# The attention bias kept with reversed rows, and the mLSTM gates computed feature-major

## The reference

```python
yc, yl = even_mixer(hc @ ev_w_in, hl @ ev_w_in, na_rpb, ml_conv_w, ...)
# split of the 3088 columns: NA q, k, v | mLSTM x, v, o | i gates (8) | f gates (8)
# latent attention, per grid row of 64 tokens (4 rows):
s_loc = q . k_window + rpb[head, row offset, column offset]   # window of 16 columns
s_ctx = q . k_context
p = softmax([s_loc, s_ctx]);  out = p_loc . v_window + p_ctx . v_context
# mLSTM, per head (4) and direction (2):
i_pre = zi + i_bias;  log_f = log_sigmoid(zf + f_bias)
```

## Time and profile before

| | |
|---|---|
| median of three runs | 2040.75 us |
| the profiled execution's own time | 2040.45 us |
| its span in the profile | 2038.7 us |
| mean granted clock of TensorE | 0.974 of full speed |
| busy: PE, VectorE, ScalarE, GpSimd | 96%, 62%, 32%, 14% |

### The profile page before, as it was taken

One profiled execution on the slowest core, in us unless ns is written; L12 is line 12 of the kernel. 1 busy time (PEld: TensorE's weight loads), 2 busy tenths in 40 slices (PEclk: granted clock), 3 DMA queues, 4 the chain that ended last, 5 costly groups with the idle time before them and its releaser, 6 DMA issues.

```text
span 2038.7 us, 24301 instructions
## 1 busy us (share of the span) xinstructions
PE 1950.0 (96%) x9246; PEld 1535.7 (75%) x9246; DVE 1267.0 (62%) x2231; ACT 645.4 (32%) x1093; POOL 290.4 (14%) x318
## 2 busy tenths in 40 slices
PE   6999999999999989899999999999999899989997
PEld 6888878885554454688887888888778867779997
DVE  7677776753872663677678447774677535465454
ACT  2322242323342431422224233222432332324452
POOL 0000001240000002500000122000034535130003
PEclk9999999998997999899999999999999999989999
DMA  8354536313350001245544223553234555214442
GB/s 359 123 203 169 206 139 167 128 54 124 135 217 0 1 0 42 104 170 204 203 165 167 96 114 140 207 206 123 103 115 174 208 193 189 83 42 166 178 168 108
DMA packets 43959, 290.12 MB, mean 142 GB/s; under 512 B 13916, under 2 KB 19676, under 8 KB 27232
## 3 DMA queue, kind: packets, MB, share of 16 engines
q1 hardware_dynamic: 34336, 270.08, 35.2%
q10 hardware_dynamic: 9536, 18.88, 2.4%
HBM read 272.16 MB, written 16.78 MB: 142 GB/s over the span
## 4 chain that ended last, share of the span: by engine, by line
PE 85%; DVE 7%; ACT 3%; DMA 2%; issue 1%; POOL 1%; SPq 0%; ACTq 0%; POOLq 0%; DVEq 0%
PE bank L606 13%; PE bank L611 12%; PE bank L608 12%; PE bank L663 7%; PE bank L669 6%; PE bank L672 6%; PE bank L800 4%; PE bank L797 3%; PE bank L784 3%; PE bank L981 2%; PE bank L737 2%; PE bank L890 1%; PE bank L727 1%; DMA slot<-in_down_dram 1%; PE bank L978 1%; PE bank L936 1%
## 5 line engine op out<-in xcount | busy, mean ns | idle before, releaser
L1701 DVE CUSTOM_DVE_ANT_0 L<-slot 128x1024 f32<-128x1024 f32 x272 | 337.7, 1241 | 72.1 <-DMA slot<-in_ada_dram 65.0
L1165 ACT ACTIVATE w_hi<-slot 128x1024 fp32r<-128x1024 f32 x176 | 186.2, 1060 | 572.7 <-PE bank L611 559.1
L1758 DVE TENSOR_TENSOR w_lo<-slot,w_hi 128x1024 fp32r<-128x1024 f32 x176 | 217.3, 1237 | 218.0 <-ACT w_hi L1165 212.1
L606 PE MATMUL bank<-m_hi,w_hi 128*128 128x512 f32 (+1 forms) x1344 | 296.6, 363 | 3.2 <-ACT w_hi L1165 3.2
L608 PE MATMUL bank<-m_lo,w_hi 128*128 128x512 f32 (+1 forms) x1344 | 296.1, 363 | 0.0
L611 PE MATMUL bank<-m_hi,w_lo 128*128 128x512 f32 (+1 forms) x1344 | 296.1, 362 | 0.0
L606 PEld LDWEIGHTS bank<-m_hi,w_hi 128*128 128x128 f32 x1344 | 232.3, 189 | 43.1 <-ACT w_hi L1165 4.0
L608 PEld LDWEIGHTS bank<-m_lo,w_hi 128*128 128x128 f32 x1344 | 232.5, 189 | 39.3
L611 PEld LDWEIGHTS bank<-m_hi,w_lo 128*128 128x128 f32 x1344 | 232.5, 189 | 39.3
L1917 DVE TENSOR_TENSOR down_lo<-slot,down_hi 128x1408 fp32r<-128x1408 f32 x64 | 108.6, 1710 | 129.2 <-ACT down_hi L1215 128.9
L669 PE MATMUL bank<-g_lo,down_hi 128*128 128x512 f32 (+1 forms) x770 | 156.8, 352 | 0.0
(11 more groups left out here) (345 smaller groups left out, 2658.7 us busy)
## 6 DMA issues: line engine op xcount, KB each, us to landing
slot<-in_gateup_dram SPq DMA_DIRECT2D x44, 2048.0 KB, 7.5
slot<-in_ada_dram SPq DMA_DIRECT2D x34, 2048.0 KB, 7.5
slot<-in_down_dram SPq DMA_DIRECT2D x32, 1408.0 KB, 5.9
slot<-in_ev_in_dram SPq DMA_DIRECT2D x4, 2048.0 KB, 9.7
slot<-in_od_in_dram SPq DMA_DIRECT2D x4, 2048.0 KB, 10.1
R<-s_ops SPq DMA_DIRECT2D x16, 512.0 KB, 5.8
s_tables<-slot ACTq DMA_DIRECT2D x8, 768.0 KB, 3.3
R<-s_tables SPq DMA_DIRECT2D x8, 768.0 KB, 6.1
```

The lines of the kernel that those rows point to most:

```text
L606: nc.tensor.matmul(bank[j][:, c0:T], w_hi[:, off, c, :], m_hi[:, c, c0:T], start=(c == 0), stop=False)
L1165: nc.scalar.activation(w_hi[:, off, :, :].rearrange("p a b -> p (a b)"), slots[b][:, (2 * (f % 2) + off) * D:(2 * (f % 2) + off + 1) * D], ...
L1701: ins = nc.vector.tensor_tensor_reduce(out=junk, in0=slots[k][:, t * D:(t + 1) * D], in1=csilu[s_], scale=1.0, scalar=0.0, op0=ALU.mult, o ...
L1758: nc.vector.tensor_tensor(w_lo[b][:, t, :, :].rearrange("p a b -> p (a b)"), slots[b][:, t * D:(t + 1) * D], w_hi[:, off, :, :].bitcast(F3 ...
```

## The change

1. The bias is no longer turned on PE. The add of the mask takes `bias_flipped` from SBUF and leaves the rows reversed. To suit, ScalarE writes the latent queries (tiles 8 to 11) in reversed order within each 128, VectorE's copy of the latent attention outputs reverses them back, and the mask itself is turned once, by a matmul of 64 columns right after the early modulation and a copy in ffn0.
2. The gate weights are spread by GpSimd to 128 columns, kind k at columns 32k to 32k + 3 and zero elsewhere. They are the stationary operand, and the tokens are the moving one: 8 matmuls of 128x512 give each kind at partitions 32k of bank 4. ScalarE reads them with the bias added directly into `rows`, at tile 6. The transposes and the copy of them go.

```diff
+        gate_w = slots[1][:, KT * 16:KT * 16 + KT * P].rearrange("p (c a b) -> p c a b", a=4, b=32)
 # SyncE, load of slot 2
-                            sp.wait_ge(sem("na_bias_turned"), 8)
+                            sp.wait_ge(sem("na_bias_masked"), 8)
 # PE
             early_modulation()
+            pe.wait_ge(sem("even_params_in"), 16 * 7)
+            nc.tensor.matmul(banks[7][:, 0:GRID_W], flip[:, :], na_mask[:, :], start=True, stop=True).then_inc(sem("na_mask_turned"), 1)
...
-                pe.wait_ge(sem("even_params_in"), 16 * 7)
-                pe.wait_ge(sem("na_bias_in"), 16 * ROWS * ROWS)
-                for n in range(4):
-                    turn_bias(n)
                 def gates(j):
                     if j == 0:
-                        for n in range(4, 8):
-                            turn_bias(n)
                         return
                     take(1)
-                    for t in range(TT):
-                        for c in range(KT):
-                            last = nc.tensor.matmul(banks[4][:, 16 * t:16 * t + 16], m[:, c, t * P:(t + 1) * P], gw[:, c, :], ...)
+                    pe.wait_ge(sem("gates_spread"), 2)
+                    for c in range(KT):
+                        last = nc.tensor.matmul(banks[4][:, :], gate_w[:, c, :, :].rearrange("p a b -> p (a b)"), m[:, c, :], ...)
                     last.then_inc(used[1], 1)
                 project("even", 4, 3, False, behind=gates)
-                pe.wait_ge(sem("even_gates_read"), 1)
-                for kind in range(4):
-                    for t in range(TT):
-                        last = nc.tensor.transpose(banks[4 + kind][0:HEADS, t * P:(t + 1) * P], gates_tok[:, t, 4 * kind:4 * kind + 4], ident[:, :])
-                    last.then_inc(sem("even_rows_done"), 1)
 # ScalarE, at tile 6 (the same four reads behind the silus go)
-                        nc.scalar.activation(gates_tok..., banks[4][:, 0:TT * 16], ACT.Copy).then_inc(sem("even_gates_read"), 1)
+                        for kind in range(4):
+                            nc.scalar.activation(rows[:, kind, :], banks[4][32 * kind:32 * kind + HEADS, :], ACT.Identity,
+                                                 bias=gate_b[:, kind:kind + 1]).then_inc(sem("even_rows_ready"), 1)
 # ScalarE, read of tiles 8 to 11; the context half follows as before
+                    if n < 12:
+                        turned = lambda v: v[:, CTX:T].rearrange("p (a n) -> p a n", n=P)
+                        nc.scalar.activation(turned(dst)[:, :, ::-1], turned(src), ACT.Copy, scale=NA_DIM ** -0.5)
+                        dst, src = dst[:, 0:CTX], src[:, 0:CTX]
 # VectorE: the mask adds, now all eight at the head of even()
+                dve.wait_ge(sem("na_bias_in"), 16 * ROWS * ROWS)
+                for n in range(8):
+                    nc.vector.tensor_tensor(cols(na_bias[:, n // 4, part, :]), cols(bias_flipped[:, n // 4, part, :]), mask...)
 # VectorE, in ffn0 behind the input remainders
+                    dve.wait_ge(sem("na_mask_turned"), 1)
+                    link(nc.vector.tensor_copy(na_mask[:, :], banks[7][:, 0:GRID_W]))
 # VectorE, attention output
-                nc.vector.tensor_copy(y[:, hp, a:b], banks[4 + group % 2][:, 0:CTX])
+                nc.vector.tensor_copy(dst, src if st == 0 else src[:, :, ::-1])
 # GpSimd, head of even()
+                pool.wait_ge(full[1], 16 * (uses_before("even")[1] + 1))
+                nc.gpsimd.memset(gate_w.rearrange("p c a b -> p (c a b)"), 0.0).then_inc(sem("gates_spread"), 1)
+                pool.wait_ge(sem("gates_spread"), 1)
+                nc.gpsimd.tensor_copy(gate_w[:, :, :, 0:4], slots[1][:, 0:KT * 16]...).then_inc(sem("gates_spread"), 1)
```

More of the change, by code:

```diff
@@ L268, in build @@
         probsT = view(L, 2 * T, 2, 4, 2 * P)
-        gates_tok = view(L, 6 * T, TT, 16)
+        gate_w = slots[1][:, KT * 16:KT * 16 + KT * P].rearrange("p (c a b) -> p c a b", a=4, b=32)
         rows = slots[4][0:HEADS, :].rearrange("p (a n) -> p a n", n=T)
@@ L692, in ffn @@
                 norm_stats(name, 1)
[L694 to L699, removed]
             def norm_stats(name, s_):
@@ L816, in even @@
                 project_first("even", 0, banks[0:4])
-                pe.wait_ge(sem("even_params_in"), 16 * 7)
-                pe.wait_ge(sem("na_bias_in"), 16 * ROWS * ROWS)
-                for n in range(4):
-                    turn_bias(n)
                 def gates(j):
                     if j == 0:
-                        for n in range(4, 8):
-                            turn_bias(n)
                         return
                     take(1)
-                    pe.wait_ge(sem("na_bias_masked"), 8)
-                    gw = slots[1][:, 0:KT * 16].rearrange("p (k n) -> p k n", n=16)
-                    for t in range(TT):
-                        for c in range(KT):
-                            last = nc.tensor.matmul(banks[4][:, 16 * t:16 * t + 16], m[:, c, t * P:(t + 1) * P], gw[:, c, :],
-                                                    start=(c == 0), stop=(c == KT - 1))
+                    pe.wait_ge(sem("gates_spread"), 2)
+                    for c in range(KT):
+                        last = nc.tensor.matmul(banks[4][:, :], gate_w[:, c, :, :].rearrange("p a b -> p (a b)"), m[:, c, :], start=(c == 0), stop=(c == KT - 1))
                     last.then_inc(used[1], 1)
                 project("even", 4, 3, False, behind=gates)
-                pe.wait_ge(sem("even_gates_read"), 1)
-                for kind in range(4):
-                    for t in range(TT):
-                        last = nc.tensor.transpose(banks[4 + kind][0:HEADS, t * P:(t + 1) * P],
-                                                   gates_tok[:, t, 4 * kind:4 * kind + 4], ident[:, :])
-                    last.then_inc(sem("even_rows_done"), 1)
                 project("even", 8, 2, False)
@@ L1397, in even @@
                         act.wait_ge(used[1], slot_done[1])
-                        nc.scalar.activation(gates_tok.rearrange("p a b -> p (a b)"), banks[4][:, 0:TT * 16], ACT.Copy).then_inc(sem("even_gates_read"), 1)
+                        for kind in range(4):
+                            nc.scalar.activation(rows[:, kind, :], banks[4][32 * kind:32 * kind + HEADS, :], ACT.Identity,
+                                                 bias=gate_b[:, kind:kind + 1]).then_inc(sem("even_rows_ready"), 1)
                     projected("even", n, 3)
@@ L1403, in even @@
                     nc.scalar.activation(xc[:, hd, :], xc[:, hd, :], ACT.Silu)
-                for kind in range(4):
-                    act.wait_ge(sem("even_rows_done"), kind + 1)
-                    nc.scalar.activation(rows[:, kind, :], banks[4 + kind][0:HEADS, :], ACT.Identity, bias=gate_b[:, kind:kind + 1]).then_inc(sem("even_rows_ready"), 1)
                 act.wait_ge(sem("even_rows_step"), 1)
@@ L1742, in _, with mask_bias @@
             early_modulation(ada_early[1])
[L1744 to L1750, removed]
+            def mask_bias():
+                dve.wait_ge(sem("na_bias_in"), 16 * ROWS * ROWS)
+                cols = lambda v: v.rearrange("p a (r c) -> p (a r) c", c=GRID_W)
+                for n in range(8):
+                    part = slice(2 * (n % 4), 2 * (n % 4) + 2)
+                    nc.vector.tensor_tensor(cols(na_bias[:, n // 4, part, :]), cols(bias_flipped[:, n // 4, part, :]),
                                             na_mask[:, :].unsqueeze(1).to_broadcast([P, 2 * ROWS, GRID_W]), ALU.add).then_inc(sem("na_bias_masked"), 1)
@@ L2097, in even @@
             def even():
-                mask_bias(0, 4)
+                mask_bias()
                 slot_done[:] = uses_before("even")
@@ L2105, in even @@
                 for hd in range(HEADS):
-                    if hd == 2:
-                        mask_bias(4, 8)
                     dve.wait_ge(sem("even_proj_read"), hd + 1)
@@ L2259, in attention_out @@
                 dve.wait_ge(sem("na_out_done"), 2 * group + 2)
-                nc.vector.tensor_copy(y[:, hp, a:b], banks[4 + group % 2][:, 0:CTX]).then_inc(sem("even_y0"), 1)
+                dst, src = (v.rearrange("p (a n) -> p a n", n=P) for v in (y[:, hp, a:b], banks[4 + group % 2][:, 0:CTX]))
+                nc.vector.tensor_copy(dst, src if st == 0 else src[:, :, ::-1]).then_inc(sem("even_y0"), 1)
             nc.vector.memset(ones_w[:, :], 1.0).then_inc(sem("mean_w_ready"), 1)
@@ L2414, in even @@
             def even():
+                pool.wait_ge(full[1], 16 * (uses_before("even")[1] + 1))
+                nc.gpsimd.memset(gate_w.rearrange("p c a b -> p (c a b)"), 0.0).then_inc(sem("gates_spread"), 1)
+                pool.wait_ge(sem("gates_spread"), 1)
+                nc.gpsimd.tensor_copy(gate_w[:, :, :, 0:4], slots[1][:, 0:KT * 16].rearrange("p (c a b) -> p c a b", a=4, b=4)).then_inc(sem("gates_spread"), 1)
                 nc.gpsimd.memset(L[:, 0:2560], 0.0)
```

## The result

| | before | after |
|---|---|---|
| median of the runs | 2039.88 us (2037.14 to 2041.18, 4 runs) | 2029.23 us (2026.26 to 2031.22, 4 runs) |
| ratio, 95% interval | | 0.9944 [0.9932, 0.9956] |
| the profiled execution's own time | 2040.45 us | 2031.22 us |
| span, mean granted clock | 2038.7 us, 0.974 | 2029.5 us, 0.975 |

The change makes the kernel 0.56% faster. The prediction was 2026.8 us in a range of 2021.7 to 2030.7, and the median lies in it. The profiled execution is the slowest of the four and lies 0.5 us above the range.

The account below looks back on a forecast made before the run. TensorE, busy for 96% of the span, was taken to bound the kernel. Terms 6.86 + 2.34 + 2.92 + 1.75 = 13.87 us off 2040.45 gave 2026.6, with the median's 0.30 added 2026.8, range 2021.7 to 2030.7.

Parts of the forecast that it names:

- the turns: Even mixer's projections: eight bias turns on PE, 16 records in two stretches, go; 6.86 us gained.
- the gates with the clock behind them and the transposes: Even mixer's projections: cheaper gates, full clock behind them and 16 transposes removed; 7.0 us gained together.
- The 2.34 of the gates: Gates' block on PE: 9.21 us of 16-column matmuls become 6.87 us of 128x512 ones; 2.34 us gained.
- 2.92: Tiles 6 and 7 behind the gates: 16.66 us partly at low clock become 13.74; 2.92 us gained.
- DVE's idle before its first S5 step: Row chain ahead of the S5 blocks: VectorE keeps spare time, 8.9 us where it had 7.54.
- The parameters: Mask's turn after the early modulation: seven small DMAs land near 38 us, costing nothing; if as late as 50, 2.5 us.
- POOL: GpSimd's added memset and copy ahead of its memsets: PE needs the spread weights at 461.6 us, 20 us of cover.
- Rival 1: Stretch at 473 to 483 us: the clock falls anyway, the 2.92 stay lost, 2029.7 us; chance 0.08.
- rival 2: Attention: clock stays at 1.2 GHz to its end at 716 us, costing 37 us more, 2064; chance 0.03.
- Rival 3: S5 blocks: the row chain takes the gain, 2036.9 us at most; chance 0.04 together with rival 4.
- Rival 4: Bias turns were free, PE would wait at 455 us; only 7.0 left, 2033.7; chance 0.04 together with rival 3.
- The attention's low stretch: Half clock from about 634 to 657 us, left as it is; a shorter one, 5 us gained, had chance 0.05.

Follow-up runs that it names:

- the pieces: Kernel after with the old 16-column gate matmuls in three groups behind tiles 4, 5 and 6, and the old transposes: 2033.37 us, ratio 0.9959 to the kernel before.
- the bias part alone: Kernel after, but with the old gate matmuls and their 16 transposes: 2035.43 us, ratio 0.9971 to the kernel before.
- the doubled block: Kernel after with the gates' 8 matmuls issued twice in the same place: 2035.14 us, ratio 0.9968 to the kernel before, 6.3 us more than after.
- the second: Trace of the unchanged kernel after, measured again in more runs: 2028.86 us, ratio 0.9934 to the kernel before.
- the gates part alone: Kernel before with only the new gates, the bias turns kept: 2034.66 us, ratio 0.9963 to the kernel before.
- the control: Kernel after with four 16-column matmuls in each of the three places in the attention's opening that held full-length ones: 2028.11 us, ratio 0.9935 to the kernel before.

## Why the prediction was right

**The sum.** 13.87 were forecast for the touched stretch and 13.8 to 13.9 came. By terms: the turns 6.86, measured alone 6.8; the gates with the clock behind them and the transposes 7.0, measured alone 7.05. Within the second half one label was wrong. The 2.34 of the gates stood there as the price of the short form; the pieces show 6.90 us at full clock. So low clock was 2.31 + 2.92 = 5.23 of the 13.87, and the form as such 0.03. The sum held because the price was read off the row where the work stood. At full clock the records took 6.90, 0.108 each. The rule that the prediction took from the Trainium skill ("TensorE: Matmul & The Clock Gate", section "Step-by-step: what each phase is for"), that the time of a matmul is its streamed columns, would have made them 0.86, and the traces do not bear it out for matmuls this short.

**What had to keep pace.** DVE's idle before its first S5 step is 8.77 us (8.9 forecast). Its mask adds took 5.72 (5.5) and started at 430.13. The two halves of ACT's read of the queries, one of them written backwards, take 0.36 to 0.38 us each, 0.63 to 0.67 from the start of the first to the end of the second against 0.60 before; DVE's copies of the attention's outputs keep their 0.42. The parameters came at 38.85 (38 forecast) and the first FFN matmul stayed at 47.6. The one miss is POOL, whose weights were ready at 439.8, where the rows of before would put them near 436: its gains (the layer norm's scale and shift, `L2388`) ran beside DVE's adds and took 11.35 us instead of 7.38. Twenty-two microseconds of cover hid it.

**The rivals.** Rival 1 is out: the clock is 1.00 from 440 to 610. So is rival 2, the clock came back in the attention. Rival 3 would have left DVE without idle time, and it has 8.77. Rival 4 is refuted by the bias part alone, 0.9971 [0.9960, 0.9983], and by the doubled block, which cost 6.3 of its 6.9 us.

**What was short.** The medians are 2.4 and 2.1 us above the forecast, within its range. The terms are in the traces, and the sum had neither: the mLSTM is 2.7 us longer, and the waits for down weights in the last FFN are 2.0 longer in the first trace and 0.8 in the second. Of the attention the start was measured 13.8 earlier and the length 0.6 shorter. The mLSTM took 65.06 us in the traces of before and of both halves alone, 67.7 to 68.0 in eight others in which nothing of it was edited, and 64.7 and 70.6 in one each; what decides between them wasn't settled, nor whether the change itself brings the longer one about. The attention's low stretch stayed at 23.9 us as assumed, on the ground that PE's work ahead of it doesn't change. In the traces of both halves that work doesn't change either, and the stretch is 6.8. With the short one the kernel would come out near 2022 (an estimate from the 6.9 us between them), still within the range: that the medians lie as near the forecast as they do is in this part luck.

## What to carry to other kernels

Price work to be removed from its own rows and look at the granted clock over it and behind it: here 5.2 of 13.9 us were not instructions but half clock, which came in a run of short matmuls on a PE that never idled. Where short matmuls open a stage, a few unread full-length matmuls in waits that are there anyway are worth a try: three gave 8.8 us here (2020.05 against 2028.86, 8.4 by the ratios), one alone and further ones elsewhere nothing that is clear of the scatter.

## What the runs showed of the hardware

- PE went to half clock without idling before it: in the control it was busy for 10.00 of 10.00 us at 0.66 and then 0.50. Full-length matmuls in the same places, for about the same time, kept 1.00 in the first window; the second has 0.83, one low piece of 3.4 us.
- The same instructions stand in a long or a short low stretch from one trace to the next: 23.9 us in the attention of before, 6.8 in that of the gates part alone, 6.9 us of time. That it also differs between executions of one program is inferred: the runs of either half spread over 9 to 10 us, and the fastest is the one whose trace has the short stretch.
- GpSimd's eight gains of 128x512 (SBUF to SBUF) took 11.35 us, on average 1.42 each, where DVE's adds of two SBUF operands ran beside the later ones, and 7.38, 0.92 each, before. With the bias part alone, which has the adds, they took 11.34, with the gates part alone, which has not, 7.35. The Trainium skill ("SBUF — State Buffer", section "Who interferes with whom") says that a VectorE instruction with two SBUF inputs contends with GpSimd instructions that read SBUF; the trace agrees.
- Reversed access cost nothing visible: ACT's 128x256 halves stay at 0.36 to 0.38 us whether or not they are written backwards, and DVE's 128x256 copies from PSUM, half of them read backwards, at 423 to 425 ns (424 to 426 before).
